# Query splits, compressed scores and sampled transposes moved among the compression's tiles

## The reference

```python
def compress(rows, pe, w1, b1, w2):          # overlapping blocks of 32 rows, every 16 rows
    blk = rows[:, idx] + pe[:, None, :]
    hid = gelu(einsum('bclgd,ldh->bcgh', blk, w1) + b1)
    return einsum('bcgh,hd->bcgd', hid, w2)
...
kc, vc = compress(keys), compress(values)
p_c = masked_softmax(q @ kc * scale, c_end <= q_pos);  o_c = p_c @ vc
o_s = attention over the selected blocks of 64 (16 of them: here all blocks up to the query's)
o_w = attention over a window of 512
out = g0 * o_c + g1 * o_s + g2 * o_w          # gates: sigmoid of a projection of x
```

## Time and profile before

| | |
|---|---|
| median of 3 runs | 1760.28 us (1758.5 to 1761.78) |
| the profiled execution | 1756.2 us, span of its instructions 1754.6 us |
| TensorE busy | 1630.3 us, 93% of the span |
| VectorE, ScalarE, GpSimd busy | 998.3, 716.6, 303.0 us |
| mean granted TensorE clock | 0.959 |
| compression tiles 4 to 7 | 132.6 to 160.9 us |
| prompt attention | about 180 to 378 us |

### The profile page before, as it was taken

One profiled execution on the slowest core, in us unless ns is written; L12 is line 12 of the kernel. 1 busy time (PEld: TensorE's weight loads), 2 busy tenths in 40 slices (PEclk: granted clock), 3 DMA queues, 4 the chain that ended last, 5 costly groups with the idle time before them and its releaser, 6 DMA issues. The chain is left out here.

```text
span 1754.6 us, 31439 instructions
## 1 busy us (share of the span) xinstructions
PE 1630.3 (93%) x12602; PEld 1585.8 (90%) x12602; DVE 998.3 (57%) x1551; ACT 716.6 (41%) x1308; POOL 303.0 (17%) x758
## 2 busy tenths in 40 slices
PE   8998898987998999999998998799899999999986
PEld 8997777866998999999998998799899999999985
DVE  3344476764786435535557595758753454355562
ACT  4444475862444324313334346434442342233341
POOL 4610242440032102102200000001320121021000
PEclk9999699997999999999999999899899999999998
DMA  7744000033212222222231222131222222222211
GB/s 259 134 137 150 1 1 1 1 116 127 74 60 86 89 79 95 86 85 85 86 104 58 90 74 84 54 117 61 73 85 91 78 97 85 85 85 99 81 61 64
DMA packets 39947, 148.01 MB, mean 84 GB/s; under 512 B 6305, under 2 KB 6321, under 8 KB 39361
## 3 DMA queue, kind: packets, MB, share of 16 engines
q1 hardware_dynamic: 33264, 121.26, 21.3%
q0 software_dynamic: 6544, 24.81, 4.2%
HBM read 140.57 MB, written 9.10 MB: 85 GB/s over the span
## 5 line engine op out<-in xcount | busy, mean ns | idle before, releaser
L1805 PE MATMUL PS<-XH,HI 128*128 128x272 f32 (+1 forms) x1936 | 412.4, 295 | 40.7 <-DVE XL L1089 14.1
L1805 PE MATMUL PS<-XH,LO 128*128 128x272 f32 (+1 forms) x1936 | 405.5, 291 | 0.0
L1805 PE MATMUL PS<-XL,HI 128*128 128x272 f32 (+1 forms) x1936 | 404.9, 291 | 0.0
L1805 PEld LDWEIGHTS PS<-XH,HI 128*128 128x128 f32 x1936 | 311.3, 192 | 44.7 <-DVE LO L448 23.4
L442 ACT ACTIVATE HI<-RAW 128x1024 fp32r<-128x1024 f32 x223 | 235.4, 1057 | 283.0 <-PE PS L1805 259.0
L1805 PE MATMUL PS<-GH,HI 128*128 128x272 f32 (+1 forms) x1504 | 320.1, 295 | 23.2 <-DVE LO L448 8.3
L448 DVE TENSOR_TENSOR LO<-RAW,HI 128x1024 fp32r<-128x1024 f32 x223 | 272.3, 1222 | 102.3 <-ACT HI L442 97.0
L1805 PE MATMUL PS<-GH,LO 128*128 128x272 f32 (+1 forms) x1504 | 315.0, 291 | 0.0
L1805 PE MATMUL PS<-GL,HI 128*128 128x272 f32 (+1 forms) x1504 | 314.2, 290 | 0.0
L1805 PEld LDWEIGHTS PS<-XL,HI 128*128 128x128 f32 x1936 | 309.9, 191 | 0.1
L1805 PEld LDWEIGHTS PS<-XH,LO 128*128 128x128 f32 x1936 | 307.9, 191 | 0.0
(11 more groups left out here) (359 smaller groups left out, 1962.6 us busy)
## 6 DMA issues: line engine op xcount, KB each, us to landing
RAW<-in_w_stream SPq DMA_DIRECT2D x223, 512.0 KB, 3.3
ARENA<-in_cache_cmp POOLq DMA_DIRECT2D x32, 128.0 KB, 3.0
out_win_old<-in_win_copy POOLq DMA_DIRECT2D x1, 4064.0 KB, 19.2
X<-in_x SPq DMA_DIRECT2D x4, 544.0 KB, 7.1
X<-in_x POOLq DMA_DIRECT2D x1, 2176.0 KB, 9.2
out_y<-X POOLq DMA_DIRECT2D x1, 2176.0 KB, 6.9
ARENA<-in_cache_sel POOLq DMA_DIRECT2D x16, 128.0 KB, 2.9
ARENA<-in_cache_win POOLq DMA_DIRECT2D x4, 512.0 KB, 5.3
```

The lines of the kernel that those rows point to most:

```text
L1805: ins = mm(PS[0:rows, b + h, 0:width], w[:, 0:rows], cols(x, x0 + n, h), start=first, stop=last)
```

## The change

- The eight high parts of the queries are written in ScalarE's steps 3 and 4 (`q_hi`), under a semaphore of their own (`q_split`), ahead of the key copies; the low parts in VectorE's steps 3 and 4.
- The sampled transposes stand behind tile 4, in banks 4 and 5 only, and their copies to `VM` in ScalarE's step 4.
- `cmp_scores(0)` stands behind tile 6 and `cmp_scores(1)` behind tile 7; `cmp_mask(0)` in VectorE's step 6.
- The value products come after that, in banks 1, 3 and 5 (`compressed`). Their copies and subtractions stand among the first exponentials and reciprocals.
- The meeting of all engines ahead of attention is gone; TensorE waits for single semaphores in its place, and the first two exponentials for the value products (`w2_done` 2).

```diff
@@ ScalarE @@
+            def q_hi(at):
+                for j in range(at, at + 4, 2):
+                    for gg in range(2):
+                        rows = slice(64 * gg, 64 * gg + 64)
+                        s.activation(QS2[gg][rows, j:j + 2, :], QF[rows, j:j + 2, :], ACT.Copy).then_inc(q_split, 1)
...
                 if n == 3:
+                    q_hi(0)
                     act.wait_ge(tr_done, 1)
...
                 if n == 4:
+                    q_hi(4)
                     act.wait_ge(kv_out, 32)
...
-                if n in (4, 6):
-                    for j in range(2 * n - 8, 2 * n - 4, 2):
-                        for gg in range(2):
-                            rows = slice(64 * gg, 64 * gg + 64)
-                            s.activation(QS2[gg][rows, j:j + 2, :], QF[rows, j:j + 2, :], ACT.Copy).then_inc(qk_hi, 1)
-                if n == 7:
-                    act.wait_ge(w2_done, 2)
-                    vm = VM[0:32, :].rearrange("p (h c) -> p h c", h=2)
-                    chain.did(s.activation(vm, PS[0:32, 6:8, :], ACT.Copy))
...
+                    act.wait_ge(tr_done, 2)
+                    for r in (32, 64):
+                        ins = s.activation(VM[r:r + 4, :].rearrange("p (h c) -> p h c", h=2), PS[r:r + 4, 4:6, :], ACT.Copy)
...
-            ins.then_inc(phase_end, 1)
-            at_phase(act, 1)
+
+            def compressed_values():
+                act.wait_ge(w2_done, 2)
+                act.wait_ge(vcz_clear, 1)
+                for r in range(4):
+                    ins = s.activation(VCZ[32 * r:32 * r + 32, 64 * r:64 * r + 64],
+                                       PS[32 * r:32 * r + 32, 5, 64 * (r % 2):64 * (r % 2) + 64], ACT.Copy)
...
+            def compressed_sampled():
+                vm = VM[0:32, :].rearrange("p (h c) -> p h c", h=2)
+                chain.did(s.activation(vm[:, 0, :], PS[0:32, 1, :], ACT.Copy))
+                s.activation(vm[:, 1, :], PS[0:32, 3, :], ACT.Copy).then_inc(w2_took, 1)
+                act.wait_ge(w2_took, 3)
...
             cmp_exp(0)
+            compressed_values()
             exps(0)
             exps(1)
+            compressed_sampled()
@@ VectorE @@
-                        dve.wait_ge(qk_hi, 4 + j + gg + 1)
+                        dve.wait_ge(q_split, j + gg + 1)
...
                     if n == 5:
                         dve.wait_ge(w2_done, 1)
-                        q_lo(0)
...
                 if n == 3:
+                    q_lo(0)
                     dve.wait_ge(w2_took, 1)
...
+                if n == 4:
+                    q_lo(4)
+                if n == 6:
+                    cmp_mask(0)
                 if n == 5:
                     dve.wait_ge(qk_hi, 4)
...
-            q_lo(4)
-            dve.wait_ge(w2_took, 2)
...
-            at_phase(dve, 1)
...
-            cmp_mask(0)
             neg_max(0)
             neg_max(1)
+            chain.sync()
             cmp_scale(0)
             one_over_sum(0)
+            compressed_values()
             one_over_sum(1)
@@ TensorE @@
+                if n == 4:
+                    pe.wait_ge(w2_took, 1)
+                    pe.wait_ge(qk_lo, 8)
+                    for row, tl in ((32, 3), (64, 5)):
+                        for b in range(NB):
+                            ins = mm(PS[row:row + 4, 4 + b // 4, (b % 4) * P:(b % 4 + 1) * P],
+                                     KS[:, tl * 32 + 4 * b:tl * 32 + 4 * b + 4], IDENT[:, :], start=True, stop=True)
+                    ins.then_inc(tr_done, 1)
+                if n == 6:
+                    pe.wait_ge(q_split, 8)
+                    pe.wait_ge(qk_lo, 13)
+                    cmp_scores(0)
+                if n == 7:
+                    cmp_scores(1)
+
+            def compressed():
+                pe.wait_ge(hid_ready, 4)
+                pe.wait_ge(tr_took, 2)
...
-            at_phase(pe, 1)
...
-            cmp_scores(0)
+            compressed()
+            pe.wait_ge(qk_hi, 4)
+            pe.wait_ge(qk_lo, 17)
+            wait_taken(pe, O0["cmp"] + 7)
             scores(0)
             scores(1)
-            cmp_scores(1)
             for u in range(64):
                 n = u // 4
+                if u == 2:
+                    pe.wait_ge(w2_took, 3)
```

More of the change, by code:

```diff
@@ L780, in _ @@
[L780 to L785, removed]
-            ins.then_inc(phase_end, 1)
-            at_phase(act, 1)
+                    act.wait_ge(tr_done, 2)
+                    for r in (32, 64):
+                        ins = s.activation(VM[r:r + 4, :].rearrange("p (h c) -> p h c", h=2), PS[r:r + 4, 4:6, :], ACT.Copy)
+                        if r == 32:
+                            chain.did(ins)
@@ new lines, in _ @@
+                    ins.then_inc(tr_took, 1)
+            def compressed_values():
[4 more added lines that the diff above has]
+                                       PS[32 * r:32 * r + 32, 5, 64 * (r % 2):64 * (r % 2) + 64], ACT.Copy)
+                    if r < 3:
+                        chain.did(ins)
+                ins.then_inc(w2_took, 1)
@@ L1811, in _, with cmp_scores @@
                      each=(lambda k: pe.wait_ge(in_lo, k + 1)) if n == 0 else None)
+            def cmp_scores(c):
+                i = CMP_BLOCKS[c]
+                for j in range(NJ):
+                    for gg in range(2):
+                        for x in range(2):
+                            ins = mm(PS[:, 6 + c % 2, 64 * j + 32 * gg:64 * j + 32 * gg + 32],
+                                     QS2[gg][:, j, i * P:(i + 1) * P], KCD[:, x, gg, :], start=x == 0, stop=x == 1)
+                ins.then_inc(sc_done, 1)
             for n in range(8):
@@ L1861, in _ @@
-            for r in range(4):
-                for gg in range(2):
-                    for hh in range(2):
-                        ins = mm(PS[32 * r:32 * r + 32, 5, gg * HD:gg * HD + HD],
-                                 HPR[:, hh * 64 + gg * 32:hh * 64 + gg * 32 + 32],
-                                 W2[:, 128 + hh * 64:128 + hh * 64 + 64], start=hh == 0, stop=hh == 1)
-            ins.then_inc(w2_done, 1)
-            pe.wait_ge(w2_took, 2)
-            pe.wait_ge(qk_hi, 12)
-            pe.wait_ge(qk_lo, 21)
```

88 lines of the change are left out of this document (40 added, 48 removed).

## The result

| | before | after |
|---|---|---|
| median | 1760.01 us (1758.5 to 1761.78, 4 runs) | 1740.05 us (1737.33 to 1749.05, 4 runs) |
| ratio | | 0.9895, 95% interval 0.9858 to 0.9932 |
| profiled execution (span) | 1756.2 (1754.6) us | 1739.8 (1738.2) us |
| mean granted clock | 0.959 | 0.964 |

The account below looks back on a forecast made before the run. TensorE, 93% busy, was taken as the bound, alternating between waits and half clock before attention. Waits 9.4, transposes 1.3, scores 2.5, value products 1.6, score matmuls 0.7, less 3.3, plus fill: 1760.3 - 12.6 = 1747.7 us, range 1743 to 1754.

Parts of the forecast that it names:

- T: Moment at which TensorE has issued both scores(0) and scores(1) at the start of attention; forecast at 178.3 us.
- the way from T to the first transposes: Maxima, scaling, reciprocal and GpSimd products before attention's first transposes, no longer covered by compressed scores: 4.0 us.
- The two dips: Half-speed clock behind each moved score group, 3.3 us each, losing 1.7 in tile 7 and 1.7 in the value products.
- Rival 1: No clock dips behind the moved score groups, or only one: T at 174.9 to 176.6, time 1744.3 to 1746.0; chance 0.17.
- Rival 2: Longer dips behind the second scores, or loop dips falling less well: 5 to 8 us remain, 1752 to 1755; chance 0.18.
- Rival 3: Moved transposes don't count as work, so tile 5 runs 3.3 us at half speed: 1749.4; inside the forecast's 0.58.
- Rival 4: Low clock holds from the transposes to T: 33.4 us more, T near 208, time 1777; chance 0.07, whole or in part.
- Rival 5: First query copies delay key copies over 2.7 us, so transposes wait behind tile 4: 1748 to 1751; inside the forecast's 0.58.
- check sum: Itemised gain from compression to attention: waits 9.4, transposes 1.3, scores 2.5, value products 1.6, score matmuls 0.7, less 3.3: 12.2 us.
- Transposes and their two waits: Sampled transposes leave the chain before attention: waits of 3.0 and 2.1 us go, the transposes themselves gain 1.3.
- The score move: Compressed scores moved behind tiles 6 and 7: 2.5 us gained after dips, 2.2 us wait covered, 3.3 us uncovered after T.
- The query splits: Query copies and subtractions moved into steps 3 and 4, removing TensorE's wait before tile 7: 2.1 us saved.

Follow-up runs that it names:

- the second set: The changed kernel timed again, unedited: 1746.63 us in 6 runs, ratio 0.9936 to the kernel before; its profiled execution took 1743.9 us.
- keys_later: Changed kernel with the key stage moved behind tile 4 and the sampled transposes behind tile 5: 1738.44 us (4 runs), ratio 0.9876 to the kernel before.
- fused: Changed kernel with both groups of compressed scores in a row behind tile 7, the first mask after them: 1749.1 us, ratio 0.9952 to the kernel before.
- doubled: Changed kernel with the first group of compressed scores issued twice behind tile 6, 64 matmuls for 32: 1752.32 us, ratio 0.9963 to the kernel before.
- interleaved: Changed kernel with the first score group spread through tile 6, four matmuls ahead of each of eight steps: 1741.85 us, ratio 0.9899 to the kernel before.

## Why the prediction was wrong

- **Which waits go, and what hides the moved work: right.** Queries, key copies, transposes, sampled copies, masks all lay beside tiles as laid out; no new wait appeared before T. The key subtractions ended at 136.9 (forecast 136.5), KKH at 149.9 (149.6), the sampled copies at 152.0 (151.7).
- **The stages' prices: right.** Score groups 3.6 each as taken, value products 4.8 (4.9), transposes 3.2 (3.6), the way from T to the first transposes 3.4 (4.0), to the second 4.5 (5.2).
- **The two dips: the step that failed.** The prediction charged both as certain, 1.7 us each, 3.4 us of clock lost in tile 7 and in the value products. In the first profile neither came: tile 7 took 6.5 us and the value products 4.8 us, both at 1.00. T was 175.1 in place of 178.3, and with the way after T the loop stood 16.5 us earlier in place of 12.6; of these 3.9 us, 3.4 are the dips and the rest small prices. Rival 1 had T at 174.9; its mechanism is the one the first profile shows. Where both dips come the sum is right: the second profile took 45.3 us from tile 4's start to T, the forecast 45.8. Three profiles of the changed kernel had none, two and none, those of its variants none to two. So the error is to charge in full what comes in about half of the places, from one place in the loop.
- **The set of four: a draw, 3.6 us.** 12.6 + 3.9 + 3.6 = 20.1, against 20.0 measured. The last term is no step of the mechanism. The prediction took its gain from the median, 4.1 us above the profiled execution of the kernel before, which was a quick draw (attention 190.2, where a second execution has 193.8). The first profile of the changed kernel was as quick (1739.84, attention 190.3), but in that set its median stood only 0.2 us above it. Over all 16 runs it stands 4.3 above (1744.1), and 1760.3 - 16.5 = 1743.8: taken from the median, the gain without dips fits them within their uncertainty of 2 us. That this set came out at 1740 is luck, or the chip; the runs don't say which.
- **The range: too narrow below.** It ended at rival 1 plus a little, for a median of few runs of a kernel that scatters by 4.4 us. Over all 16 runs the gain is 15.3 us (1759.4 to 1744.1), which the forecast misses by 2.7; the second set alone gave 12.7.
- **Rival 2** (longer low clock in the loop) exists: behind unit 29's group the low clock lasted 3.4 us in three executions (attention 190.2 to 190.3) and 10 us and more in the others (193.1 to 195.9), in most of them from before the group on. It belongs to both kernels. A longer dip behind the second scores, as the rival had it, is in none of the changed kernel's three profiles but in three of its variants' (6.8 us). **Rival 3**, that the transposes don't count as work: the clock stayed at 1.00 through them (table by stage, first row) and in tile 5. The Trainium skill (TensorE: Matmul & The Clock Gate, Part 4: PE-mode transpose) says of transpose-mode that the full clock doesn't engage; these are ordinary matmuls against the identity, and the trace shows no such thing for them. **Rival 4**, that the low clock holds from the transposes on, was never seen. **Rival 5**: the key copies were 1 us later, as found.
- **What the parts were worth, by the items of the check sum.** Transposes and their two waits: 3.0 + 2.1 + 1.3 = 6.4, measured 7.2, uncertain by 2 to 3. The score move: 2.5 after its dips, 2.2 covered, 3.3 uncovered, net 1.4; measured 0.4 to 0.8, or 3.4 within the set, so open. The query splits: 2.1, measured 3.2 to 6.2: an item that was too small, since the prediction gave that wait no clock to win. A wait that goes can give more than itself if the clock then stays up in what follows.

Left open: what decides whether a dip comes, why the low clock lasts 3.4 us at one time and 10 to 17 at another around the same group, whether the two heaps go with the execution or with the set, and whether keys_later keeps its lead in more runs.

## What to carry to other kernels

Price a wait of TensorE with the clock of the work behind it, and a group of sparse matmuls with the low clock that it may bring, as something that comes in part of the executions and not as a fixed term. Before comparing one profile with a median, look whether the profiled execution is an ordinary one: compare its stages with a second profile, above all those that the change doesn't touch. Don't read four runs of a kernel that scatters by 4 us as its time. Keep a group of sparse matmuls short: the two profiles with 64 in a row both lost the clock for 10 us. Spreading it through dense work (interleaved) and covering a wait with a dense tile (keys_later) gave the lower medians here, but that they do better isn't shown.

## What the runs showed of the hardware

- A stream of matmuls that keeps TensorE 100% busy by the profile can pull its clock down: 128 x 128 weights with 32 moving columns, 0.111 us each at 2.4 GHz and 0.21 at 1.2. With 64 of them in a row it fell 4.5 us (fused) and 4.9 us (doubled) after the first, one profile each. Behind or inside a single 32 between dense tiles or ahead of the value products it fell in 8 of 17 places.
- Once down, the clock stayed so for 3.4 us (five times) or 6.8 us (three times) at a single group in these places, and for 10 us with 64 in a row, in doubled for 6 us into a dense tile, with TensorE 100% busy.
- The time of the same program goes with the mean clock: 16 runs of the changed kernel from 1737.3 to 1750.7, with mean clocks from 0.965 to 0.959, while the variant with both score groups back in attention (scores_back) stayed within 3.1 us in ten runs.
